# Near scores of an HGRN2 scan packed in one PSUM bank and spread by transfers, with three smaller edits around them

## The reference, cut to what matters

```python
def hgrn2_chunked(q, k, v, log_f):
    # S_t = diag(f_t) S_{t-1} + k_t v_t^T (k_t = 1 - f_t), o_t = S_t^T q_t
    bc = jnp.cumsum(gc, axis=-2)
    ...
        diff = bi[..., :, None, :] - bi[..., None, :, :]
        decay = jnp.exp(jnp.where(causal, diff, -jnp.inf))
        scores = jnp.einsum("bhtd,bhsd,bhtsd->bhts", qi, ki, decay)
        o = (jnp.einsum("bhts,bhsv->bhtv", scores, vi)
             + jnp.einsum("bhtd,bhdv->bhtv", qi * jnp.exp(bi), state))
```

## Time and profile before

| | |
|---|---|
| median of 3 runs | 1417.77 us (1417.52 to 1419.52) |
| the profiled execution | 1420.56 us, span 1418.8 us |
| busy over the span | PE 1401.1 us (99%), DVE 1031.2 (73%), ACT 704.5 (50%), POOL 226.1 (16%) |
| instructions | 20665 |
| mean granted TensorE clock | 0.995 |
| up to 418.20 us | the projections (`Front`), PE busy 415.04 |
| 418.20 to 556.93 us | the scan, PE busy 131.31, DVE 126.93, ACT 118.64, POOL 118.03 |
| behind 556.93 us | the projection, the MLP and the rest, PE busy 854.77 |

### The profile page before, as it was taken

How to read it: one execution, slowest core, us unless ns; L and a number is a source line. 1 busy time by engine, 2 the same in 40 slices (tenths; PEclk the granted TensorE clock), 3 DMA queues, 4 the chain that set the end, 5 groups by cost and what they waited for, 6 DMA issues and landing times.

```text
span 1418.8 us, 20665 instructions
## 1 busy us (share of the span) xinstructions
PE 1401.1 (99%) x7683; PEld 1171.1 (83%) x7683; DVE 1031.2 (73%) x1522; ACT 704.5 (50%) x1309; POOL 226.1 (16%) x239
## 2 busy tenths in 40 slices
PE   9999999999999999999999999999999999999998
PEld 8877888888878998888888888888888888888886
DVE  7594545562148997368988999999999686577567
ACT  6343456422258896258653344343435444454455
POOL 4000001101038885010000000000000254400000
PEclk9999999999999999999999999999999999999999
DMA  7431323544623332645342344334327765424223
GB/s 241 105 74 30 45 80 116 154 112 108 166 72 108 121 120 83 216 149 184 105 126 82 119 136 139 111 104 160 108 89 259 240 195 196 135 82 134 90 61 148
DMA packets 153251, 181.06 MB, mean 128 GB/s; under 512 B 21241, under 2 KB 92095, under 8 KB 153152
## 3 DMA queue, kind: packets, MB, share of 16 engines
q1 hardware_dynamic: 153152, 179.74, 40.8%
HBM read 130.43 MB, written 49.28 MB: 127 GB/s over the span
## 4 chain that ended last, share of the span: by engine, by line
PE 93%; DVE 3%; ACT 1%; issue 1%; DMA 1%; POOL 0%; SPq 0%; DVEq 0%; ACTq 0%; POOLq 0%
PE psum L2468 9%; PE psum L2470 9%; PE psum L2469 9%; PE psum L2407 5%; PE psum L2408 5%; PE psum L2409 5%; PE psum L674 4%; PE psum L676 4%; PE psum L675 4%; PE psum L2380 4%; PE psum L2381 4%; PE psum L2382 4%; PE psum L1373 3%; PE psum L734 3%; PE psum L732 3%; PE psum L733 3%
## 5 line engine op out<-in xcount | busy, mean ns | idle before, releaser
L166 DVE TENSOR_TENSOR w_wlo<-w_raw,w_whi 128x1024 fp32r<-128x1024 f32 x66 | 86.8, 1317 | 228.1 <-ACT w_whi L151 228.0
L151 ACT ACTIVATE w_whi<-w_raw 128x1024 fp32r<-128x1024 f32 x66 | 69.7, 1058 | 175.4 <-PE psum L2382 79.0
L3201 DVE TENSOR_TENSOR g_slot<-w_raw,g_slot 128x512 fp32r<-128x512 f32 x77 | 69.5, 902 | 51.6 <-ACT g_slot L2775 51.5
L2775 ACT ACTIVATE g_slot<-w_raw 128x512 fp32r<-128x512 f32 x77 | 48.7, 632 | 104.8 <-PE psum L2409 99.6
L674 PE MATMUL psum<-h_hi,w_whi 128*128 128x512 f32 x256 | 100.6, 393 | 0.0
L676 PE MATMUL psum<-h_hi,w_wlo 128*128 128x512 f32 x256 | 99.7, 390 | 0.0
L675 PE MATMUL psum<-h_lo,w_whi 128*128 128x512 f32 x256 | 99.7, 389 | 0.0
L3459 POOL TENSOR_TENSOR mixed_home<-mixed_home 128x512 f32<-128x512 f32 x11 | 16.0, 1455 | 507.0 <-DMA mixed_home<-in_w_down 505.0
L2380 PE MATMUL psum<-w_whi,m_hi 128*128 128x512 f32 x224 | 87.8, 392 | 0.0
L2382 PE MATMUL psum<-w_whi,m_lo 128*128 128x512 f32 x224 | 87.2, 389 | 0.0
L2381 PE MATMUL psum<-w_wlo,m_hi 128*128 128x512 f32 x224 | 87.2, 389 | 0.0
(11 more groups left out here) (446 smaller groups left out, 3967.0 us busy)
## 6 DMA issues: line engine op xcount, KB each, us to landing
w_raw<-in_w_up SPq DMA_DIRECT2D x39, 512.0 KB, 4.0
w_raw<-in_w_in SPq DMA_DIRECT2D x36, 512.0 KB, 6.2
s_rows<-pair_work SPq DMA_DIRECT2D x11, 1024.0 KB, 4.1
w_raw<-s_rows SPq DMA_DIRECT2D x44, 256.0 KB, 2.7
g_rows<-pair_work SPq DMA_DIRECT2D x18, 512.0 KB, 2.6
w_raw<-g_rows SPq DMA_DIRECT2D x33, 256.0 KB, 4.2
w_raw<-in_w_out SPq DMA_DIRECT2D x16, 512.0 KB, 4.1
mixed_home<-in_w_down SPq DMA_DIRECT2D x32, 256.0 KB, 4.4
```

## The change

1. **Levels 0 to 5** are multiplied in blocks of 32 keys, four for each head, by 16 queries (level 0: by 32). All six lie side by side in bank 0 (`near_part`). Level 0 moves behind `pe_hgrn` of the chunk before. VectorE merges the six under masks of 32 columns into a new packed tile `near` (`dve_near`), each waiting for the one in front of it. Level 6 is copied beside them, level 7 straight into the scores.
2. **Transfers** spread the packed tile: four from `near` into `s_h_scores`, one for each 32 partitions (`sp_unpack`), issued from SyncE's queue behind the load of `at`. `pe_hgrn` waits for all four.
3. **The first decay** (level index 0) is 1 - k from the keys, one copy by ScalarE; no difference, and no key product on GpSimd. **The last** (index 6) is made by ScalarE from the cumulated decay with the middle as its bias, a pair of instructions for each head; no difference.
4. **The root** is exp(-0.5 ln(x)) on ScalarE, out of one table set that is loaded once; the reciprocal on VectorE goes.
5. **The query product** moves from GpSimd to VectorE (`dve_query`).
6. **The inverse**: `y32` and `dt32` are multiplied in two halves of 64 rows, `dx` on the upper 64 rows alone, `y64` and `dt64` over 64 rows; `dve_dx` copies 32 rows without a mask.
7. Masks for the near levels are built once by GpSimd ahead of the scan; one of the old masks goes.

```diff
+    NEAR_BANK, SCORE_BANK = 0, {6: 1, 7: 7}
+    NEAR, MIDDLE = LEVELS - 2, P // 2 - 1
...
-    DT_ROWS, Y64_ROWS = (slice(0, P - SB), slice(0, 2 * SB)), slice(2 * SB, P)
+    DT_ROWS, Y64_FROM, Y64_ROWS = (slice(0, P - SB), slice(0, 2 * SB)), slice(0, 2 * SB), slice(2 * SB, P)
...
+    def near_part(self, ap, n):
+
+        at, width = (0, SB) if n == 0 else (NH * SB + (n - 1) * NH * SB // 2, SB // 2)
+        return ap[:, at:at + NH * width].rearrange("p (h t) -> p h t", h=NH)
+
+    def near_heads(self, c):
+        return self.near[c % 2][:].rearrange("p (h t) -> p h t", h=NH)
...
+    def sp_unpack(self, sp, c):
+
+        self.banks.released(sp, ("score", c, LEVELS - 1))
+        self.banks.released(sp, ("near", c))
+        if c:
+            self.done(sp, ("oh", c - 1))
+        sc, near = heads(self.sc[:]), self.near_heads(c)
+        for b in range(P // SB):
+            rows, width = slice(b * SB, (b + 1) * SB), SB if b % 2 else 2 * SB
+            sp.dma_start(sc[rows, :, b * SB:b * SB + width], near[rows, :, 0:width]).then_inc(self.s["unpacked"], 16)
...
                 self.load_part(sp, "at", c + 1, self.at)
+            self.sp_unpack(sp, c)
+            if c + 1 < NT:
                 self.done(sp, ("hd", c))
                 self.load_rows(sp, "v", c + 1, 2 * DG, self.hv)
...
+    def pe_halves(self, pe, key, bank, left, right, side):
+
+        out = self.banks.open(pe, key, bank)
+        for h in range(NH):
+            for half in range(2):
+                rows = slice(half * 2 * SB, (half + 1) * 2 * SB)
+                cols = slice(rows.start + side * SB, rows.start + (side + 1) * SB)
+                ins = pe.matmul(self.hs(out, h)[rows, cols], left(h)[rows, rows], right(h)[rows, cols], start=True, stop=True)
+        self.multiplied.mark(ins, key)
...
+        if n <= self.NEAR:
+            out = self.near_part(self.banks.of(("near", c)), n)
             for h in range(NH):
-                for b in range(P // size):
-                    part = slice(b * size, (b + 1) * size)
-                    ins = pe.matmul(hs(out, h)[part, part], kk[:, h, part], q[:, h, part], start=True, stop=True)
-            self.multiplied.mark(ins, ("score", c, n))
+                for b in range(P // SB):
+                    keys, queries = slice(b * SB, (b + 1) * SB), slice(b * SB // 2, (b + 1) * SB // 2)
+                    left = hs(self.kl[at], h)[:, keys] if n > 1 else kk[:, h, keys]
+                    right = self.packed(self.ql[at])[:, h, queries] if n else q[:, h, keys]
+                    ins = pe.matmul(out[keys, h, :], left, right, start=True, stop=True)
+        else:
+            out = self.packed(self.banks.open(pe, ("score", c, n), self.SCORE_BANK[n]))
+            for h in range(NH):
+                for b in range(P // (2 * ahead)):
+                    keys = slice(2 * b * ahead, (2 * b + 1) * ahead)
+                    ins = pe.matmul(out[keys, h, 0:ahead], hs(self.kl[at], h)[:, keys],
+                                    self.packed(self.ql[at])[:, h, b * ahead:(b + 1) * ahead], start=True, stop=True)
+        self.multiplied.mark(ins, ("score", c, n))
...
-        for n in range(1, LEVELS + 1):
-            self.banks.released(pe, ("score", c, n))
+        pe.wait_ge(s["unpacked"], (c + 1) * (P // SB) * 16)
+        self.banks.released(pe, ("score", c, LEVELS))
...
+        if lv in (0, LEVELS - 1) and n >= 3:
+            act.wait_ge(self.s["levels"], n - 2)
+        if lv == 0:
+            act.wait_ge(self.front.s["bounded"], 2 * NH)
+            ins = act.activation(self.blocks(heads(ed[:]), m, 1), self.blocks(self.part(self.front.kk, c), m, 1), ACT.Copy,
+                                 scale=-1.0, bias=1.0)
+        elif lv == LEVELS - 1:
+            b = self.part(self.front.f, c)
+            act.wait_ge(self.s["middles"], 1)
+            for h in range(NH):
+                at = c * NH + h
+                act.activation(self.hs(ed, h)[:, 0:m], b[:, h, 0:m], ACT.Exp, scale=-1.0, bias=b[:, h, m - 1:m])
+                ins = act.activation(self.hs(ed, h)[:, m:P], b[:, h, m:P], ACT.Exp, bias=self.middle[:, at:at + 1])
+        else:
+            act.wait_ge(self.s["differed"], c * self.NEAR + lv)
+            act.activation(side(ed[:], 0), side(ed[:], 0), ACT.Exp, scale=-1.0)
+            ins = act.activation(side(ed[:], 1), side(ed[:], 1), ACT.Exp)
         ins.then_inc(self.s["expd"], 1)
...
-            act.wait_ge(self.s["inverted"], 2 * c - 1)
-        act.activation(self.column(1), self.column(0), ACT.Sqrt, bias=self.k.eps[:, 0:1],
+            act.wait_ge(self.s["inverted"], c)
+        act.activation(self.column(1), self.column(0), ACT.Ln, bias=self.k.eps[:, 0:1],
                        scale=1.0 / HD).then_inc(self.s["rooted"], 1)
+        act.wait_ge(self.s["rooted"], 2 * c + 1)
+        act.activation(self.column(2), self.column(1), ACT.Exp, scale=-0.5).then_inc(self.s["rooted"], 1)
...
+    def dve_near(self, dve, c):
+
+        self.done(dve, ("score", c, self.NEAR))
+        if c >= 2:
+            dve.wait_ge(self.s["unpacked"], (c - 1) * (P // SB) * 16)
+        bank, blocks = self.banks.of(("near", c)), self.near_heads(c)[:, :, 0:SB]
+        for n in range(self.NEAR + 1):
+            if n:
+                dve.wait_ge(self.s["placed"], c * self.NEAR + n)
+            mask, m = self.k.near[:, n, :].bitcast(U32), 1 << max(n - 1, 0)
+            mask = mask.unsqueeze(1).broadcast_to([P, NH, SB])
+            data = self.near_part(bank, n)
+            if n:
+                side = lambda ap: self.blocks(ap, m, 1)
+                ins = dve.copy_predicated(side(blocks), side(mask), data.rearrange("p h (n m) -> p h n m", m=m))
+            else:
+                ins = dve.copy_predicated(blocks, mask, data)
+            if n == self.NEAR:
+                self.banks.release(ins, ("near", c))
+            else:
+                ins.then_inc(self.s["placed"], 1)
...
+        if n == LEVELS:
+            if c:
+                self.done(dve, ("oh", c - 1))
+            ins = dve.tensor_copy(heads(self.sc[:])[0:ahead, :, ahead:P], data)
         else:
-            ins = dve.copy_predicated(heads(self.sc[:]), over_heads(k.ident[:].bitcast(U32)), heads(self.banks.of(key)))
+            ins = dve.tensor_copy(self.near_heads(c)[0:P - ahead, :, SB:2 * SB], data)
         self.banks.release(ins, key)
...
+    def dve_query(self, dve, c):
+        dve.wait_ge(self.s["q_decay"], c + 1)
+        if c == NT // 2:
+            self.front.queries(dve, 1)
+        here = heads(self.hqd[:])
+        dve.tensor_tensor(here, here, self.part(self.front.q, c), ALU.mult).then_inc(self.s["queried"], 1)
...
         for c in range(NT):
             more = c + 1 < NT
             if c:
                 self.dve_dx(dve, c)
-            if c:
                 self.dve_differ(dve, c, 3)
-            self.dve_place(dve, c, 0)
-            if c == 0:
+            else:
                 dve.memset(self.state[:], 0.0)
                 dve.memset(self.hstate[:], 0.0).then_inc(s["cleared"], 1)
                 dve.wait_ge(s["cleared"], 2)
             if c:
                 self.dve_hstate(dve, c - 1)
-            self.dve_place(dve, c, 1)
-            if c:
                 self.dve_differ(dve, c, 4)
                 self.dve_rhs(dve, c)
-            self.dve_place(dve, c, 2)
-            if c:
                 self.dve_differ(dve, c, 5)
                 self.dve_dt(dve, c, 1)
-            self.dve_differ(dve, c, 6)
-            self.dve_place(dve, c, 3)
-            if c:
                 self.dve_outputs(dve, c - 1)
-            self.dve_place(dve, c, 4)
-            self.dve_differ(dve, c + 1, 0)
-            self.dve_place(dve, c, 5)
+            self.dve_near(dve, c)
             self.dve_differ(dve, c + 1, 1)
             self.dve_place(dve, c, 6)
             if c:
@@ -1841,6 +1916,7 @@
                 self.slabs.remainder(dve, self.front.first["q"] + NH + 1)
             if more:
                 self.dve_state(dve, c)
+            self.dve_query(dve, c)
             self.dve_place(dve, c, 7)
```

More of the change, by code:

```diff
@@ L1274, in __init__ @@
             self.on = t("normed", DM)
+            self.near = [t(f"h_near{i}", DG // 2) for i in range(2)]
+            self.middle = t("h_middle", NT * NH)
             self.junk = t("junk", P, mybir.dt.bfloat16)
@@ L1372, in pe_products @@
         for h in range(NH):
-            ins = pe.matmul(columns(self.hs(out, h)), left(h)[:, rows], columns(right(h)), start=True, stop=True)
+            ins = pe.matmul(columns(self.hs(out, h)), left(h)[inner, rows], columns(right(h)[inner]), start=True, stop=True)
         self.multiplied.mark(ins, key)
@@ L1425, in pe_score @@
         kk, q = self.part(self.front.kk, c), self.part(self.front.q, c)
-        if n:
-            pe.wait_ge(s["levels"], c * LEVELS + n)
-            at = (c * LEVELS + n - 1) % 3
-            out = self.banks.open(pe, ("score", c, n), self.SCORE_BANK[n])
-            size = self.block_of(n)
```

(55 more changed lines are left out.)

76 lines of the change are left out of this document (37 added, 39 removed).

## The result

The changed kernel takes 1439.93 us (median of 4 runs, 1438.12 to 1440.61), the kernel before 1418.64 us beside it: a ratio of 1.0147, 95% interval 1.013 to 1.0165. It is 1.5% slower. The forecast of 1419.6 us and its range up to 1431 missed it; "slower" had the largest chance, 0.40.

A forecast was written before the change was run, and what follows sets the result against it. TensorE was taken to set the pace, VectorE close behind. Stretches 5.21 + 5.95 + 2.87 + 3.78 made a chunk of 17.81 us, 0.42 more; with the ends +1.8 us: 1419.6 us, range 1409 to 1431.

The forecast's parts named there:

- D: Stretch from level 7's start to `pe_hgrn`, set by the unpacking transfers: 3.78 us in place of 2.65 (2.9 to 4.8).
- the term with the widest ends: Landing of the unpacking transfers within SBUF, in the stretch ahead of `pe_hgrn`: 2.0 us, with ends of 1.3 and 2.8.
- The narrow one: Three further unpacking issues on SyncE, 0.36 to 0.48 us apart, taken as 0.42 each: 1.26 us.
- The clock, the rival with 0.22: TensorE's clock falls at the new gaps ahead of `pe_hgrn`; four falls cost 6.6 us: 1426 us. Chance 0.22.
- 0.12: Chance of the rival with late transfers or blocks costing 0.51 us: a chunk of 18.8, some 1428 us.
- the change touches only the scan: The sum is made only in the scan, from 418.2 to 556.9 us of the span.
- A: Stretch from `pe_hgrn` to level 2 on TensorE: 5.21 us in place of 4.99.
- B: Stretch from level 2 to `gd`, set by ScalarE, `gd` waiting for `act_vn`: 5.95 us (5.6 to 6.4), from 6.88.
- C: Stretch from the state product `gd` to level 7: stays 2.87 us.
- The floor for small matmuls: Rival: each small matmul has a minimum cost, 0.8 us a level, chunk 19.9 us, 1434 us. Chance 0.04.
- The last chunk: No loads before its unpacking: 6.7 us to level 6's placing, then 3.3; 10.0 in place of 11.82, -1.8 us.
- the full relief: VectorE's relief comes through whole: 15 us a chunk, 1402 us; a few hundredths of the quick-transfers rival's 0.23.

The follow-up runs named there:

- the idle products: The changed kernel with eight idle TensorE products in the gap ahead of `pe_hgrn`, which waits as before: 1431.33 us, ratio 1.0092.
- the returned square root: The changed kernel with GpSimd copies for transfers, `act_vn` before the last decay, query product and level 7 before the state, and the square root back: 1414.93 us.
- the copies on GpSimd alone: The changed kernel with the four unpacking transfers replaced by four copies on GpSimd and nothing else: 1414.78 us, ratio 0.998.
- the best version: The changed kernel with GpSimd copies for transfers, `act_vn` ahead of the last decay, query product and level 7's placing ahead of the state: 1412.36 us.
- the early transfers: The changed kernel with the four unpacking transfers ahead of the load of `at` in SyncE's queue: 1423.12 us, ratio 1.0025.
- early transfers with both orders: The changed kernel with transfers ahead of `at`'s load, `act_vn` ahead of the last decay, query product and level 7's placing ahead of the state: 1422.43 us.

## Why the prediction was wrong

The total first, in the profiled executions, 1439.57 us against the 1422.4 forecast on that scale, 17.2 too little. The first `pe_hgrn` starts at 436.75 (forecast 436.16 + 0.9 = 437.1: -0.3). The next six chunks take 118.65 us against 103.95 + 2.5: +12.2. The last takes 17.44 against 16.82 + 0.2 - 1.8 = 15.2: +2.2. Behind it lie 864.7 us of the span in place of 861.9: +2.8, of which 1.6 is a fall at 573.3 and 1.2 a table load (below). The time around the span is 0.3 longer. That the first `pe_hgrn` comes out so near is luck: from the issue of `at` to it 4.53 us passed where 3.67 were forecast, and that issue came at 432.22 where it was at 433.39 before, which the forecast did not have.

**D, the step that failed.** As the prediction put it: 0.11 + 0.36 + 1.26 + 2.0 + 0.05 = 3.78. In the chain above it is 0.10 + 0.43 + 1.93 + 1.82 + 0.20 = 4.48. Landing with its hand-over is 2.02 where I had 2.05, so the term with the widest ends was right. The narrow one was wrong: three issues at 0.42, taken from the loads of `x` behind `lt`, cost 0.64 each (0.60 and a pause of 0.04), 1.93 in all where the sum has 1.26. I had given that term ends of 0.36 to 0.48 by the rows of other transfers and bounded only the landing by rows of another kind; the issue of a transfer that no row showed needed the same doubt. In some chunks an issue takes longer (2.82 us for the four at 490.18, 3.46 at 510.49), which makes D 4.77 in the undisturbed chunk. There the forecast chunk of 17.81 is 18.68: with six such chunks +5.2 of the +12.2, and another 0.4 because the forecast added its 0.42 a chunk, reckoned from the 17.39 of one chunk, to the six of 103.95, whose mean is 17.33. Of the last chunk's +2.2 the issues make 0.6.

**The clock, the rival with 0.22.** It "decides when the gap comes near 2 us". The gap was forecast at 1.6 and came out at 2.06 to 3.10, because of the term above, and the clock fell behind seven of eight. By the undisturbed chunk's 18.68 the first six chunks lost 118.65 - 6 x 18.68 = 6.6 us to the five falls in them, 1.3 each (the D of this chunk is 4.77 where the mean of the six is 4.68, so the split is good to half a microsecond), and the idle products gave back 8.6 us of the run time. A fall was priced at half of 3.3 us, which was near, but four were counted and seven came. The two causes were not separate cases of 0.22 and 0.12: one follows from the other, so both belong in one rival, near 1436 (1419.6 + 7 x 0.9 + 7 x 1.5). The range, which took them one at a time, was too narrow at its upper end.

How far 2 us decides can be read from the waits ahead of `pe_hgrn` in nine kernels (the changed one and eight of its variants, all but the idle products and the returned square root), 72 waits or starts without one: a fall behind 17 of 19 waits of 2.0 us or more, behind 12 of 30 between 1.0 and 2.0, and behind none of 23 under 1.0. So 1.6 us, the forecast gap, was not safe either: by these counts some three falls in eight chunks, 4 to 5 us, belonged in the sum itself. The Trainium skill ("TensorE: Matmul & The Clock Gate", Why this matters for your kernels) advises against idle gaps between bursts of matmuls, but only against gaps longer than nearly all of these. The traces agree that falls come behind idle gaps, since the idle products removed them; they also show falls behind gaps well under that length, so here the counts decide.

**Behind the scan, a term put at nothing.** The prediction makes its sum inside the scan, as "the change touches only the scan". But the exchange of the root (point 4) moves a table load out of it. In the kernel before, the last chunk's square root left its table loaded, and the first square root of `Tail` (L2581, at 609.42) ran at once. Now the table of logarithm and exponential is loaded, and that square root has a load in front of it; the split of the weights behind it on ScalarE (L151) and VectorE (L166) is late by that much, and TensorE waits:

```profile
626.97 1.28 ACT L2651 ACT_TABLE_LOAD   x1
...
PE psum L2450 <- DVE w_wlo L166: 0.9, 1, 0.9
```

From the last `pe_hgrn` to the end it is 861.9 us in the two kernels with the square root (the one before and the returned root) and 863.0 to 863.2 in the seven with the logarithm that had no fall behind that point: +1.2.

**A, B and C** were right to 0.1 us in the chunk without a fall, with all that carries them: levels of 32 records go four abreast (0.35 taken), `y32` 0.58, ScalarE's eight last-decay instructions 0.24 apart and the wait of `gd` for `act_vn` (0.39), which moving `act_vn` gave back at 3.5 us a run. The floor for small matmuls did not show: the levels of 32 records are what rules it out. The row that the prediction set against it did not, as 0.38 us for 16 records makes 0.76 for 32, nearly the 0.8 of that rival; giving it only 0.04 was bolder than that row allows.

**The last chunk.** From level 2 to level 6's placing 6.6 us (6.7 forecast), then 4.0 to `pe_hgrn` (3.3 forecast, the issues again): 10.6 in place of 10.0. The saving of 1.2 us that is left was eaten by a fall in its stretch A.

**The reading as a whole.** "Work taken from three engines is given back at one wait" is what happened, and the experiments show both halves: the wait was the loss (the copies on GpSimd alone go from 1439.9 to 1414.8 us) and the relief had a worth that only shows without it (ScalarE's root: 0.2 us a chunk in the kernel before, 0.75 in the best version). I had said that the full relief needs the unpacking ahead of `og`; the early transfers show that this is not enough, as four issues and a landing, some 4.9 us, then follow level 6's placing. What it needed was an engine that copies at once, and in this stretch that is GpSimd: VectorE's copies wait for GpSimd's products.

Open: why the issue of these transfers costs 0.60 us where a load costs 0.32. Their size is not it, since 16 and 32 KB cost the same; the number of pieces or the tile that is read could be, and no run here tells them apart. Nor does one show why now and then an issue takes up to 1.6 us, which loads in the same kernels do as well (1.33 at 480.33, 1.48 at 526.09). Points 3, 5 and 6 of the change were not tried alone.

## What to carry to other kernels

Before moving a copy to a transfer, price three things and not one: the issues of its pieces one behind the other on the queue that has to send them, the landing, and what the queue does ahead of them; a short copy on an engine with room (here 1.9 us on GpSimd against 4.0 of issues, landing and hand-over) can be the cheaper one though it costs busy time. Where a new wait opens an idle gap of 1 to 2 us on TensorE, the price of the gap and that of the clock are one case, so take them together in the range. When a copy goes to VectorE or GpSimd, look at what the other of the two does at that time. An engine's relief that is worth nothing measurable alone (the root in the kernel before) should be tried again when the bound has moved. And where a table load is saved in a loop, look behind the loop for the instruction that used the table left by it.

## What was not expected of the hardware

- The issue of a transfer between two tiles in SBUF (128 pieces, 16 or 32 KB) takes SyncE 0.60 us, up to 1.6, where a load of 256 KB mostly takes 0.32 to 0.43; directly behind four of them (the early transfers) the load of `at` takes 0.59 to 1.11 as well.
- Such a transfer lands in 1.8 to 1.9 us where no load is near (the last chunk), and as the fourth of a set in the changed kernel; the first and second behind a load of 256 KB take 1.9 to 3.2.
- A copy of 32 partitions by 128 or 256 elements between tiles in SBUF takes VectorE 0.22 to 0.28 us while GpSimd is idle. Beside GpSimd's products it ends 0.1 to 0.2 us behind the end of one of them and takes up to 0.92. GpSimd needs 0.29 to 0.39 for it, in some places 0.64 to 1.17.
- Matmuls with 32 stationary columns in four blocks that write different quarters of the partitions take 9 to 13 ns a record.
- A fall of the clock behind a wait of `pe_hgrn` mostly lasted 3.4 us at 1.2 GHz and cost some 1.3 us; one came at a wait of TensorE of 1.1 us (early transfers with both orders, 519.69), while other waits of 1.7 us had none.
- A table load on ScalarE takes 1.28 us; one that came to stand behind the scan cost 1.2 us of the run.
